# A transformer layer with recurrent mixing and expert retrieval on one core: table bias in one load, unpadded queries, loads moved a stage ahead, fronts of blocks mixed with one-hot turns, dense sums held in PSUM

## What is computed

```
z = x @ w_in
A = sliding-window attention(q, k, v)      window 128, 16 heads, 4 kv heads, T5 bias, sinks
B = RWKV-7 time mixing(rwkv part of z)     sequential state per head of 64
mix = (sigmoid(gate_a) * (A @ w_branch_attn) + sigmoid(gate_b) * (B @ w_branch_rwkv)) @ w_out
h = LayerNorm(alpha * x + mix)
y = LayerNorm(alpha * h + PEER(h))
PEER: q = h @ peer_q; s = q . keys (8 heads, two halves, 128 keys each)
      top 16 of each half, the top 16 of their sums -> 8*16 expert indices, softmax gates
      act = gelu(peer_u[idx] . h); out = sum of gate * act * peer_v[idx]
```

## Time and profile before

| | us |
|---|---|
| median of 3 runs | 5067.17 (5052.31 to 5070.40) |
| profiled execution, its time | 5065.86 |
| its span in the trace | 5064.1 |
| PE busy, DVE busy, POOL busy, ACT busy | 3909.5, 3425.6, 1622.6, 972.7 |
| `e_` part: plain, pairs, scan, attend, merge, fronts | 170, 190, 266, 143, 95, 197 |
| `l_` part: plain, pairs, scan, attend, decode, merge | 292, 366, 512, 181, 84, 208 |
| rest of the background behind merge; fronts | 112; 661 |
| experts: start, 16 chunks, end | 63, 1474, 50 |

### The profile page before, as it was taken

The page is one execution under the profiler, slowest core; times in us unless marked ns, Lnnn a source line. Parts: engine busy times, 40 slices in busy tenths (PEclk is TensorE's granted clock), DMA queues, the critical chain, the costliest instruction groups (busy, mean ns, idle before and its releaser), DMA issues. The chain is left out here.

```text
span 5064.1 us, 71382 instructions
## 1 busy us (share of the span) xinstructions
PE 3909.5 (77%) x27756; PEld 2599.9 (51%) x27756; DVE 3425.6 (68%) x6297; ACT 972.7 (19%) x1961; POOL 1622.6 (32%) x1514
## 2 busy tenths in 40 slices
PE   9979757849987688858482567573999999899986
PEld 5448644636655477746351345462544444454442
DVE  0464531358799577769467593854889888988896
ACT  0223230001132223325110042542000000010000
POOL 0120000026433232222156000001555666666563
PEclk9989878879998799968596757565999999999997
DMA  4441135159865456554478511215999999999995
GB/s 143 150 145 55 58 54 182 76 215 357 321 216 207 175 198 203 177 176 128 161 298 312 198 58 59 96 55 212 357 386 386 391 387 403 357 398 400 385 368 203
DMA packets 384495, 1152.68 MB, mean 228 GB/s; under 512 B 49019, under 2 KB 121045, under 8 KB 380800
## 3 DMA queue, kind: packets, MB, share of 16 engines
q0 software_dynamic: 206976, 756.37, 38.9%
q1 hardware_dynamic: 163300, 372.78, 21.1%
...
## 5 line engine op out<-in xcount | busy, mean ns | idle before, releaser
L2240 PE MATMUL x_vps<-x_v,x_w 128*128 128x512 f32 x1536 | 692.5, 612 | 90.2 <-DVE x_w L2298 90.2
L2230 PE MATMUL x_sps<-k_hT,x_u 128*128 128x384 f32 x2048 | 671.0, 489 | 62.0 <-ACT x_w L2271 40.7
L329 POOL DMA_INDIRECT w_ring<-u_rows,k_eidx x384 | 491.3, 1279 | 458.9 <-DVE w_dots L374 351.1
L2230 PEld LDWEIGHTS x_sps<-k_hT,x_u 128*128 128x128 f32 x2048 | 390.8, 191 | 342.5 <-issue 53.3
L2240 PEld LDWEIGHTS x_vps<-x_v,x_w 128*128 128x128 f32 x1536 | 300.8, 197 | 475.9 <-issue 367.3
L391 DVE SCALAR_TENSOR_TENSOR w_yacc<-w_ring,w_wts,w_yacc 128x1024 f32<-128x1024 f32 x384 | 493.4, 1285 | 54.1 <-DMA w_ring<-v_rows,k_eidx 41.6
L374 DVE CUSTOM_DVE_ANT_0 w_ring<-w_ring,w_h 128x1024 f32<-128x1024 f32 x384 | 448.7, 1220 | 36.0 <-DMA w_h<-s_h 27.2
L329 POOL DMA_INDIRECT w_ring<-v_rows,k_eidx x384 | 421.2, 1097 | 137.2 <-issue 113.7
L329 POOL DMA_INDIRECT l_w_ring<-u_rows,k_eidx x256 | 287.1, 1122 | 542.9 <-DVE l_w_dots L374 209.1
L374 DVE CUSTOM_DVE_ANT_0 l_w_ring<-l_w_ring,l_w_h 128x1024 f32<-128x1024 f32 x256 | 306.2, 1224 | 96.9 <-DMA l_w_ring<-u_rows,k_eidx 66.0
L329 POOL DMA_INDIRECT l_w_ring<-v_rows,k_eidx x256 | 283.0, 1106 | 210.1 <-DVE l_w_yacc L391 79.2
...
## 6 DMA issues: line engine op xcount, KB each, us to landing
x_u<-u_cols SPq DMA_DIRECT2D x128, 512.0 KB, 7.5
x_v<-v_rows SPq DMA_DIRECT2D x128, 512.0 KB, 8.2
...
```

What stands on the lines that cost most here:

```text
L329: pool.indirect_dma_start(out=self.ring[:, r, :], out_offset=None, in_=self.A[table], in_offset=bass.IndirectOffsetOnAxis(ap=idx[:, s:s + ...
L2230: mm = pe.matmul(sps[n % 2][:, 0:ND * P], u[n % 4][:, k, :], hT[:, k, :], start=(k == 0), stop=(k == KT - 1))
L2240: mm = pe.matmul(vps[m % 2][:, x * 512:(x + 1) * 512], w[:, e, k * P:(k + 1) * P], v[:, e, x * 512:(x + 1) * 512], start=(e == 0), stop=(e ...
```

## The change

1. The bias table is made and written to HBM at the end of `e_` `project_plain` instead of in `attend`; SP waits there for its landing (`tab_out`). In both `attend` stages the bias is one load of 2 MB in the place of 16, behind the kv loads and the first two query loads; queries have no zero half, and the scores matmul contracts over 64 rows.
2. A shared SBUF region `sb_big` holds xT, aT, the dense blocks' hT and eight scan tiles. `w_out` is loaded into an own tensor in `e_` `merge` (i = 2, 4 MB), and the second part's xT in `e_` `fronts` (`x_ahead`, 8 loads, 2.6 MB).
3. `fronts` of `e_`: choose(0, 0..7) is placed before norm(2), the others behind; PE does mix(2) before ask(1), ACT the square root for norm(2) before ask(1).
4. `beside["groups"]`: 23 groups in `l_` `project_plain` in place of 19 (`u % 8` for `u % 4`); fewer are left behind `merge`.
5. `fronts` of `l_`: the pieces of blocks 2k+1 and 2k+2 are spread over the turns of k; choose(k+1, ...) is done two parts a turn in turns 16 to 31.
6. `experts`: each dense block has its own PSUM sum `x_vps[k]` over all 16 chunks; alpha and the add are three DVE instructions at the end.

```diff
@@ project_plain, end of SP's program
+                sp.wait_ge(tab_done, 1)
+                sp.dma_start(A["tab"], tab[:, :].unsqueeze(1).broadcast_to([NH, P, 3 * WIN])).then_inc(tab_out, 16)
+                sp.wait_ge(tab_out, 16)
@@ attend, SP
-            for h in range(NH):
-                src = bass.AP(A["tab"].tensor, h * P * 3 * WIN + WIN - 1, [[3 * WIN - 1, P], [1, 2 * WIN]])
-                sp.dma_start(bias[:, h, :], src).then_inc(bias_in, 16)
+            for j in range(NBUF):
+                load_q(j)
+            src = bass.AP(A["tab"].tensor, WIN - 1, [[3 * WIN - 1, P], [P * 3 * WIN, NH], [1, 2 * WIN]])
+            sp.dma_start(bias[:, :, :], src).then_inc(bias_in, 16)
@@ attend, PE
-                        mm = pe.matmul(scp[s % 2][:, x, :], q[j % NBUF][:, t, h, :],
-                                       kT[:, u // 2, j * WIN:(j + 2) * WIN], start=True, stop=True)
+                        o = slice(h * HD, (h + 1) * HD)
+                        mm = pe.matmul(scp[s % 2][:, x, :], q[j % NBUF][o, t, :],
+                                       kT[o, u // 2, j * WIN:(j + 2) * WIN], start=True, stop=True)
@@ merge, SP
+                if pt.first and i == 2:
+                    for k in range(KT):
+                        sp.dma_start(A["sb_wo"][:, k, :], A["w_out"][k]).then_inc(wo_in, 16)
@@ fronts, PE, in turn q of dense block k, behind scatter(k, q)
+                a, b = 2 * k + 1, 2 * k + 2
+                if q < 2 and b < NF:
+                    mix(b, q)
+                if q == 2 and a < NF:
+                    turned(a)
+                if 3 <= q < 11 and a < NF:
+                    query(a, q - 3)
+                if 11 <= q < 13 and a < NF:
+                    scores(a, q - 11)
+                if q == 13 and b < NF:
+                    turned(b)
+                if 14 <= q < 22 and b < NF:
+                    query(b, q - 14)
+                if 22 <= q < 24 and b < NF:
+                    scores(b, q - 22)
+                if 24 <= q < 26 and b + 1 < NF:
+                    mix(b + 1, q - 24)
@@ fronts, DVE
             for k in range(NSC):
+                if k and 2 * k + 1 < NF:
+                    norm(2 * k + 1)
                 for q in range(TURNS):
                     scatter(k, q)
-                    if k + 1 < NPK:
-                        choose(k + 1, q)
-                for i in (2 * k + 2, 2 * k + 3):
-                    if i < NF:
-                        norm(i)
+                    if q == 6 and 2 * k + 2 < NF:
+                        norm(2 * k + 2)
+                    if k + 1 < NPK and q >= 16:
+                        choose(k + 1, 2 * (q - 16))
+                        choose(k + 1, 2 * (q - 16) + 1)
@@ experts, PE
-                    m = ND * c + k
-                    if m >= 2:
-                        pe.wait_ge(S["v_read"], m - 1)
...
-                            mm = pe.matmul(vps[m % 2][:, x * 512:(x + 1) * 512], w[:, e, k * P:(k + 1) * P], v[:, e, x * 512:(x + 1) * 512],
-                                           start=(e == 0), stop=(e == CH - 1))
+                            mm = pe.matmul(vps[k][:, x * 512:(x + 1) * 512], w[:, e, k * P:(k + 1) * P], v[:, e, x * 512:(x + 1) * 512],
+                                           start=(c == 0 and e == 0), stop=(c == NCH - 1 and e == CH - 1))
@@ experts, ACT
-            act.wait_ge(S["acc_in"], 16 * ND)
-            act.activation(acc[:, :, :], acc[:, :, :], ACT.Copy, scale=ALPHA).then_inc(S["acc_begun"], 1)
@@ experts, DVE
-                mark(V.tensor_tensor(acc[:, k, :], acc[:, k, :], vps[m % 2][:, :], ALU.add), S["v_read"], m + 1)
...
+                mark(V.scalar_tensor_tensor(acc[:, k, :], acc[:, k, :], ALPHA, vps[k][:, :], ALU.mult, ALU.add), S["summed"], k + 1)
@@ program
-    beside = {"groups": lambda u: 1 if u >= 4 and u % 4 else 0, ...
+    beside = {"groups": lambda u: 1 if u >= 4 and u % 8 else 0, ...
```

More of the change, by code:

```diff
@@ L501, in _ @@
                     natural(u - 1)
+            if pt.first:
+                pe.wait_ge(tab_in, 32)
+                pe.wait_ge(ones_done, 1)
+                pe.matmul(tp[0][0:NH, 0:3 * WIN], relb[:, :], oneh[:, :], start=True, stop=True).then_inc(tab_psum, 1)
             if pt.dec:
@@ L528, in _ @@
                 bg.act(act, plan["groups"](u))
+            if pt.first:
+                act.wait_ge(tab_psum, 1)
+                act.activation(tab[:, :], tp[0][0:NH, 0:3 * WIN], ACT.Copy).then_inc(tab_done, 1)
             if pt.dec:
@@ L1779, in fronts @@
     TURNS = P // PER
-    assert picks[:NSC] == scat
+    assert picks[:NSC] == scat and (not scat or 2 * NSC + 1 >= NF)
     with ExitStack() as ctx:
@@ L1851, in _ @@
             load(1)
+            n_ahead = ahead(sp, S["ahead_in"])
             for i in range(NF):
@@ L1898, in _, with mix, turned @@
         def _(pe):
-            def mix(i):
-                pe.wait_ge(S["m_in"], 16 * i + 16)
-                if i:
-                    pe.wait_ge(S["h0_done"], i)
-                for c in range(2):
-                    for k in range(KT):
-                        mm = pe.matmul(fps[:, c * 512:(c + 1) * 512], mTb[:, k, :], wo[:, k, c * 512:(c + 1) * 512],
-                                       start=(k == 0), stop=(k == KT - 1))
-                mm.then_inc(S["mixed"], 1)
-            def ask(i):
+            def mix(i, c):
+                if c == 0:
+                    pe.wait_ge(S["m_in"], 16 * i + 16)
+                    if i:
+                        pe.wait_ge(S["h0_done"], i)
+                for k in range(KT):
+                    mm = pe.matmul(fps[:, c * 512:(c + 1) * 512], mTb[:, k, :], wo[:, k, c * 512:(c + 1) * 512],
+                                   start=(k == 0), stop=(k == KT - 1))
+                if c:
+                    mm.then_inc(S["mixed"], 1)
+            def turned(i):
                 pe.wait_ge(S["h_done"], i + 1)
@@ L1948, in _, with query, scores @@
-            pe.wait_ge(S["wo_in"], 16 * KT)
-            mix(0)
-            mix(1)
+            def query(i, x):
+                if x == 0:
+                    pe.wait_ge(S["hT_done"], i + 1)
+                for k in range(KT):
+                    mm = pe.matmul(tqps[:, x * P:(x + 1) * P], wq[:, k, x * P:(x + 1) * P], hT_of(i)[:, k, :],
+                                   start=(k == 0), stop=(k == KT - 1))
+                if x == PH - 1:
+                    mm.then_inc(S["q_psum"], 1)
+            def scores(i, c):
+                if c == 0:
+                    pe.wait_ge(S["q_done"], i + 1)
+                if 2 * i + c:
+                    pe.wait_ge(S["sc_done"], 2 * i + c)
+                for x in range(PH):
+                    mm = pe.matmul(sps[:, x * NKEY:(x + 1) * NKEY], qT[c * HD:(c + 1) * HD, x, :],
+                                   keys[c * HD:(c + 1) * HD, x, :], start=True, stop=True)
+                mm.then_inc(S["sc_psum"], 1)
@@ new lines, in ask, with scatter @@
+            def ask(i):
+                turned(i)
+                for x in range(PH):
+                    query(i, x)
+                for c in range(2):
+                    scores(i, c)
+            def scatter(k, q):
+                n = TURNS * k + q
+                if q == 0:
+                    pe.wait_ge(S["idx_done"], k + 1)
+                    if k:
+                        pe.wait_ge(S["g_done"], TURNS * k)
+                    for i, src in enumerate((ij[:, 0, :], ij[:, 1, :], gate_d[:, :, :].rearrange("p a b -> p (a b)"))):
+                        mm = pe.transpose(gps[0][:, i * P:(i + 1) * P], src, ident[:, :])
+                    mm.then_inc(S["idx_psum"], 1)
+                    pe.wait_ge(S["byslot_done"], k + 1)
+                pe.wait_ge(S["two_done"], n + 1)
+                if n >= 2:
+                    pe.wait_ge(S["g_done"], n - 1)
+                for t in range(PER):
+                    mm = pe.matmul(gps[q % 2][:, t * NKEY:(t + 1) * NKEY], one[q % 2][:, t, :], two[q % 2][:, t, :], start=True, stop=True)
+                mm.then_inc(S["g_psum"], 1)
@@ L1951, in _ @@
+            if to_load:
+                pe.wait_ge(S["wo_in"], 16 * KT)
+            for i in range(2):
+                for c in range(2):
+                    mix(i, c)
             pe.wait_ge(S["const_in"], 16 * (KT + 1))
@@ L2377, in program @@
         A["sb_STc"] = held("c_STc", [P, NPAIR, HD])
-        trunk(PARTS[0], none, nothing)
+        A["sb_big"] = held("c_big", [P, KT * max(pt.xw for pt in PARTS)])
         A["sb_eidx"] = {f: held(f"k_eidx{f}", [P, SLOTS], U32) for f in FETCHED_1 + FETCHED_2}
@@ L2386, in program @@
             trunk(PARTS[1], bg, beside)
-        A["sb_hT"] = held("k_hT", [P, KT, ND * P])
-        fronts(nc, A, "l_", [b for b in range(NB + 1) if b not in EARLY], DENSE + FETCHED_2[:1], DENSE)
+        A["sb_hT"] = wide(ND * P)
+        fronts(nc, A, "l_", [b for b in range(NB + 1) if b not in EARLY], DENSE + FETCHED_2[:1], DENSE, None, lambda sp, sem: 0)
         experts(nc, A)
```

331 lines of the change are left out of this document (158 added, 173 removed).

## The result

The changed kernel takes 4912.38 us (median of 4 runs, 4906.30 to 4913.34) beside 5068.78 for the kernel before on the same chip: a ratio of 0.9694, interval 0.9671 to 0.9718. Forecast were 4929 us, range 4865 to 5010. The profiled execution has a span of 4910.9 us, 153.2 less than before.

| stage | before | after | difference | forecast |
|---|---|---|---|---|
| e_plain | 169.1 | 199.7 | +30.6 | +34.5 |
| e_pairs, e_scan | 456.8 | 454.9 | -1.9 | 0 |
| e_attend | 142.5 | 101.7 | -40.8 | -31.6 |
| e_merge | 95.0 | 94.9 | -0.1 | +2 |
| e_fronts | 196.7 | 159.4 | -37.3 | -38 |

What follows compares the result with a forecast made beforehand. The prediction took DMA and PE as nearly full in l_plain and the experts' chunks, DVE as bounding l_pairs, and nothing as full in l_fronts. Its stage terms summed to -137 from 5065.9, giving 4929 us, range 4865 to 5010.

Steps and rivals of the forecast that it cites:

- e_fronts: First part's fronts: -38 us, bounds -30 and -44; the choice begins earlier and the wait behind w_out goes.
- l_fronts: Second part's fronts: -10 us, bounds -35 and +30; PE holds turns 0 to 15, DVE 16 to 31.
- experts: Experts stage: -12 us at the start, -48 in 14 inner chunks, -4 in the last, +2 for new DVE steps.
- three signs of being wrong: Chunks staying at 92 us, a granted clock of 0.5 in the mixed turns, or l_plain growing by 40.
- l_plain: Second part's plain projection: +26 us, bounds +5 and +40; four more groups, less xT and usable idle DMA time.
- The table and attend: Table's store and making at the end of e_plain +34.5 us, e_attend -31.6, l_attend 0.
- l_pairs, behind merge: In l_pairs -14 us from DVE's cheaper choice parts; behind merge -44 from 32 transfers gone.
- I allow 6 for slower matmuls: In l_fronts, 6 us of the counted -16 given up for slower matmuls, leaving -10.
- rival A: Chunks of experts are bound by transfers, which takes away 52 of the gain: 4981 us; chance 0.18.
- Rival B: Chunks of experts come down to 85.5 us everywhere with DVE's freed 142 us, another 39: 4890 us; chance 0.14.
- C: PE is granted 1.2 GHz throughout the mixed turns of l_fronts, +115: 5044 us, no change; chance 0.05.
- D: Turns of l_fronts serialise, costing the sum of both engines' pieces, +188: 5117 us, slower; chance 0.05.

Runs made afterwards that it cites:

- e4: Changed kernel with the bias table made beside the first plain projection and stored from POOL's queue; 4907.81 us, ratio 0.9671.
- e8: Changed kernel with e3's edit and the table made early, stored head by head in 16 stores of 192 KB; 4873.26 us, ratio 0.9597.
- e11: Changed kernel with e3's edit and the table made early, stored in one piece by POOL at the start of e_scan; 4842.58 us, ratio 0.9556.
- e12: As e11, but the table's store waits until the scan's second pair of heads is done; 4831.91 us, ratio 0.9542.
- e2: Changed kernel with 19 groups in the second part's plain projection in place of 23, four back behind merge; 4928.02 us, ratio 0.9716.
- e5: Changed kernel with the earlier fronts function for the second part, whole pieces after each 32 turns; 4954.47 us, ratio 0.9764.
- e6: Changed kernel with the dense blocks' v rows loaded for chunk 0 only, a probe with wrong sums; 4850.74 us in one run.
- e9: Changed kernel with 48 additions put back on DVE, into a spare tile and waiting for no PE product; 4949.06 us, ratio 0.9745.
- e3: Changed kernel with the choice one part per turn over all 32 turns of l_fronts, mixed pieces kept; 4841.16 us, ratio 0.9549.

## Why the prediction was right

The total is 16 us off, in part by luck: two large misses, 29 us too little for `l_fronts` and 20 too much for the experts, stand against each other, with 9 too little for `e_attend` beside them. None of the three signs of being wrong came: chunks of 88.9 us, a clock of 0.90 in the first halves, `l_plain` longer by 25.5.

- **The table and attend.** The step that moving the table buys nothing by itself is right: +30.6. e_attend gained 9 us more than I took. The bias load took 12.0 us, not the 22 of the table's store, so the first step on scores came 18 us into the stage and not 24. The other 3 us are within what the stage varies: it lasted 101 to 108 us in executions of kernels alike up to there, with granted clocks from 0.77 down to 0.69, and the kernel before had 0.70. A store of the table beside other work would not have been free: e4, e8, e11 and e12 all paid 20 us or more for it.
- **e_fronts**: -37.3 for -38, by the steps named: PE's longest wait for mT is 9.6 us for 19.9, and the choice begins 79 us into the stage, for 123 before and the 78 of the forecast.
- **l_plain**: the sum was right (+25.5 for +26), its parts were not. By e2, xT ahead was worth 16, not 6, and the groups cost 41.6 and not 32. The working took the transfers for what ended the stage with 19 groups, but PE ended it, before and in e2, so PE's start 16 us earlier counts whole there. With 23 groups PE does end 46 us before the stage, as forecast. Nor is it DMA that then ends it: the transfers run at a share of 1.03 until 1281 us, and then come 47 us in which PE has nothing to do and DVE, with the groups' choice and dot products, is busy 44.

```profile
1161.40:1281.40 120.00, 120.00 (x449) 82.21 (x448) 106.43 (x202) 14.66 (x36) 84.01 (x74) 1.00 1.03 413
1281.40:1328.60 47.20, 1.28 (x5) 0.37 (x3) 44.34 (x95) 1.43 (x5) 18.78 (x17) 0.54 0.66 247
```

- **l_pairs, behind merge**: -11 and -40.3 for -14 and -44. Taken with l_plain, moving the groups is nearly a nought sum.
- **l_fronts**: the mechanism right (PE's first halves, DVE's second), the size wrong by 29 us. The step that failed is the one with the clock: "I allow 6 for slower matmuls". The sign was wrong. Periods were 165 and 171 us for 174 and 177, and from the first turn of k = 2 to the stage's end 151 for 145 and the 11 that lie behind it. The first halves lasted 61 and 60 us, at the full-clock end of the forecast's 61 to 77, of which the sum of 174 takes 70. Before, with nothing dense between the one-hots, the clock was 0.52 and their matmuls took 433 ns; with dense work in between it is 0.90 and 298, and e5, which takes that work out again, has 0.51 to 0.53 and 433.
- **experts**: -41.7 for -62. Inner chunks came from 91.7 to 88.9, for the 88.3 forecast (-40 for -48); by e6 transfers are now the bound in most of them, which is rival A half come true. The step that failed is the rate: the forecast took 413 GB/s, and the inner chunks moved 396 on average, which for 35.2 MB is 88.9 us. The Trainium skill, "DMA: Bandwidth & Descriptors", section "Where 436 GB/s comes from", has the HBM side binding at about 358 GB/s between HBM and SBUF. This trace does not agree, on a core that runs alone: 396 GB/s in the chunks, 413 in `l_plain`. The start gave -6 for -12: PE's wait of 40.7 us for ACT was replaced by one of 34.5 for the fifth u load, the one that the forecast named. PE resumes 62 us into the stage and not 45, though with four u tiles done in the place of two. The last chunk with the end gave +4 for -2, which is not explained. My account of the chunks by DVE's waits alone was too simple: e9 shows that DVE's adds themselves are worth 31.
- Rival B is refuted by the inner chunks of 88.9 us, which it had at 85.5; C by the clock of 0.90 in the first halves. D is refuted by the halves of 61 and 104 us, which it had at 94 and 144; by e3 a small part of it is real, the two halves of a mix.
